# The fourth part of the modulation is loaded and summed during the two feed-forward layers instead of beside the values projection

## The reference

```
mod_l = silu(c) @ w_mod + b_mod                  # 6 parts of D = 2048: mod_l[0] .. mod_l[5]
hl    = modulate(rms_norm(xl, norm1_g), mod_l[0], mod_l[1])
zl    = hl @ w_in + b_in                         # projections: conv, sgu, q, k, v, gates
xl    = xl + mod_l[2] * mixer_output(...)
hl2   = modulate(rms_norm(xl, norm2_g), mod_l[3], mod_l[4])
xl    = xl + mod_l[5] * (relu(hl2 @ w_ff1 + b_ff1) ** 2 @ w_ff2 + b_ff2)
```

## Time and profile before

| | |
|---|---|
| median of 3 runs | 3076.25 us (3071.13 to 3077.77) |
| the profiled execution | 3078.38 us |
| its span on the core | 3076.6 us |
| PE busy | 3031.1 us (99%) |
| DVE busy | 1984.4 us (64%) |
| ACT busy, POOL busy | 331.5 us (11%), 63.3 us (2%) |
| DMA | 561.39 MB, 182 GB/s in the mean |
| chain that ended last | PE 88%, DVE 7%, DMA 4% |

### The profile page before, as it was taken

The page is one execution under the profiler, slowest core; times in us unless marked ns, Lnnn a source line. Parts: engine busy times, 40 slices in busy tenths (PEclk is TensorE's granted clock), DMA queues, the critical chain, the costliest instruction groups (busy, mean ns, idle before and its releaser), DMA issues.

```text
span 3076.6 us, 49684 instructions
## 1 busy us (share of the span) xinstructions
PE 3031.1 (99%) x21787; PEld 2725.3 (89%) x21787; DVE 1984.4 (64%) x2968; ACT 331.5 (11%) x643; POOL 63.3 (2%) x121
## 2 busy tenths in 40 slices
PE   6999999999999999999999999999999999999998
PEld 3688844498899999999999999999999998898998
DVE  1039975564256577766666777767667565996665
ACT  1021000022120000111110000001012102001010
POOL 0000000120000000000000000000000000000000
PEclk9999999999999999999999999999999999999999
DMA  7999977664345555755555555555445654554443
GB/s 273 308 310 299 293 245 279 224 189 131 124 138 174 169 178 178 188 166 165 192 165 165 165 165 170 170 157 189 138 143 160 198 174 124 155 145 110 123 150 111
DMA packets 580133, 561.39 MB, mean 182 GB/s; under 512 B 24317, under 2 KB 548176, under 8 KB 570445
## 3 DMA queue, kind: packets, MB, share of 16 engines
q1 hardware_dynamic: 550368, 466.65, 49.5%
q0 software_dynamic: 11552, 80.90, 7.2%
q10 hardware_dynamic: 17997, 10.67, 1.2%
HBM read 549.66 MB, written 8.51 MB: 181 GB/s over the span
## 4 chain that ended last, share of the span: by engine, by line
PE 88%; DVE 7%; DMA 4%; issue 0%; ACT 0%; SPq 0%; ACTq 0%; DVEq 0%; POOLq 0%
PE psum L487 39%; PE psum L467 20%; PE psum L764 4%; DVE arena L1954 3%; PE psum L627 2%; DVE arena L1902 2%; PE psum L565 2%; PE psum L895 2%; PE psum L883 2%; PE psum L893 2%; PE psum L888 2%; PE psum L894 2%; PE psum L885 2%; PE psum L880 2%; DMA arena<-w_mod 2%; DMA ring<-w_in 1%
## 5 line engine op out<-in xcount | busy, mean ns | idle before, releaser
L467 PE MATMUL psum<-arena,ring 128*128 128x256 f32 (+2 forms) x3712 | 870.0, 394 | 0.6 <-ACTq L1183 0.6
L467 PEld LDWEIGHTS psum<-arena,ring 128*128 128x128 f32 x3712 | 700.2, 190 | 157.0 <-issue 69.6
L487 PE MATMUL psum<-arena 128*128 128x128 f32 x6144 | 702.8, 275 | 0.3 <-DVE arena L1775 0.3
L487 PEld LDWEIGHTS psum<-arena 128*128 128x128 f32 x6144 | 694.4, 192 | 7.2 <-issue 6.2
L487 PE MATMUL psum<-arena,ring 128*128 128x128 f32 x4224 | 486.1, 275 | 0.0
L487 PEld LDWEIGHTS psum<-arena,ring 128*128 128x128 f32 x4224 | 479.1, 192 | 0.7 <-issue 0.5
L1763 DVE TENSOR_TENSOR arena<-ring 128x2048 f32<-128x2048 f32 x96 | 220.0, 2292 | 278.3 <-PE psum L487 275.9
L1902 DVE SCALAR_TENSOR_TENSOR arena<-arena,cvec 128x2048 f32<-128x2048 f32 x60 | 141.0, 2350 | 80.7 <-DMA arena<-w_mod 79.9
L1744 DVE TENSOR_TENSOR arena<-ring,arena 128x1024 f32<-128x1024 f32 (+1 forms) x168 | 167.3, 996 | 5.3
L1744 DVE TENSOR_TENSOR arena<-arena 128x512 f32<-128x512 f32 (+7 forms) x257 | 134.2, 522 | 16.2 <-DVE arena L2673 6.1
L2530 DVE TENSOR_TENSOR arena<-ring 128x1024 f32<-128x1024 f32 x64 | 78.4, 1225 | 90.3 <-PE psum L880 89.5
(11 more groups left out here) (335 smaller groups left out, 2953.4 us busy)
## 6 DMA issues: line engine op xcount, KB each, us to landing
ring<-w_ff SPq DMA_DIRECT2D x128, 1024.0 KB, 5.7
ring<-w_in SPq DMA_DIRECT2D x88, 1024.0 KB, 6.5
arena<-w_mod POOLq DMA_DIRECT2D x64, 1024.0 KB, 6.9
ring<-ab_w_in SPq DMA_DIRECT2D x56, 1024.0 KB, 5.6
ring<-cd_w_in SPq DMA_DIRECT2D x48, 1024.0 KB, 5.9
ring<-w_mod SPq DMA_DIRECT2D x32, 1024.0 KB, 7.3
ring<-w_in SPq DMA_DIRECT2D x32, 512.0 KB, 5.0
ring<-w_o SPq DMA_DIRECT2D x16, 1024.0 KB, 5.9
```

Source lines behind the costliest of these rows:

```text
L467: mm = pe.matmul(psum[:, s, m * N:(m + 1) * N], w[:, k, m * P:(m + 1) * P], x(k)[:, 0:N], start=(j == 0), stop=(j == kt - 1))
L487: return pe.matmul(o, z, w, **kw) if tokens else pe.matmul(o, w, z, **kw)
```

## The change

GpSimd's first loop loads 48 chunks instead of 64, VectorE's `chunks(16)` and its `mod_columns(3, 3)` are taken out of the place behind the values projection, and so is `mod_sum(3)` on TensorE. The fourth part is made later: each row k is loaded in two halves of 128x1024 (512 KB each) into `LATE_HALF`, and `add_late(k)` multiplies and adds the halves into `LATE`. Rows 0 to 11 follow the work of `tables` at p = 18 to 29, rows 12 to 15 follow turns i = 0 to 3 of the second feed-forward layer. TensorE's `mod_sum` for it stands behind step q = 9 of that layer, `mod_columns` at i = 5, and the bias work of p = 25 to 27 moves to i = 5 to 7. The new arrays lie where the tables of p = 17 lay, so GpSimd starts the first load only when their write to HBM has landed. The silu of c is copied to `cond` because `cvec` is overwritten in between.

```diff
-            for j in range(64):
+            for j in range(48):
...
             pool.dma_start(kept[1], at(36080, 4096)).then_inc(sem("load_tables_out"), 16)
+            pool.wait_ge(sem("load_tables_out"), 16)
+            for k in range(KT):
+                for h in range(2):
+                    pool.wait_ge(sem(f"chunk{h}_used"), n[f"chunk{h}_used"].next())
+                    c0 = 4096 + 3 * D + HW * h
+                    pool.dma_start(LATE_HALF[h], w[:, k, c0:c0 + HW]).then_inc(sem(f"load_chunk{h}"), 16)
             pool.wait_ge(sem("residual_made"), n["residual_made"].next())
             pool.dma_start(kept[0], at(0, 4096)).then_inc(sem("load_residual_out"), 16)
-            pool.wait_ge(sem("load_tables_out"), 16)
...
+            def add_late(k):
+                for h in range(2):
+                    v.wait_ge(sem(f"load_chunk{h}"), n[f"load_chunk{h}"].next())
+                    if k == 0:
+                        ins = v.tensor_scalar(LATE[:, h, :], LATE_HALF[h], cond[:, k:k + 1], None, ALU.mult)
+                    else:
+                        ins = v.scalar_tensor_tensor(out=LATE[:, h, :], in0=LATE_HALF[h], scalar=cond[:, k:k + 1],
+                                                     in1=LATE[:, h, :], op0=ALU.mult, op1=ALU.add)
+                    ins.then_inc(sem(f"chunk{h}_used"), n[f"chunk{h}_used"].up())
+                for h in range(2):
+                    v.wait_ge(sem(f"chunk{h}_used"), n[f"chunk{h}_used"].now())
+                if k == KT - 1:
+                    v.sem_inc(sem("mod_added"), n["mod_added"].up())
...
             mod_columns(2, 7)
-            chunk = chunks(16)
+            step(v.tensor_copy(cond[:, :], cvec[:, :, 0]))
             quarter_sums(HL, SM, "input_sums")
...
             pair_sums(0, w, TX)
-            mod_columns(3, 3)
...
-                elif p == 25:
-                    TT(gain[:, 1, :], mod[:, 80:96, 0], col("b_ff2", 0, KT), ALU.mult)
-                elif p in (26, 27):
-                    k = HT * (p - 26)
-                    TT(X[:, k:k + HT, :], X[:, k:k + HT, :], over(gain[:, 1, k:k + HT], T, 2), ALU.add)
+                if p >= 18:
+                    add_late(p - 18)
...
+                if i < 4:
+                    add_late(12 + i)
+                elif i == 5:
+                    mod_columns(3, 7, at(36080, KT, 32))
+                    TT(gain[:, 1, :], mod[:, 80:96, 0], col("b_ff2", 0, KT), ALU.mult)
+                elif i in (6, 7):
+                    k = HT * (i - 6)
+                    TT(X[:, k:k + HT, :], X[:, k:k + HT, :], over(gain[:, 1, k:k + HT], T, 2), ALU.add)
```

On TensorE the same four matmuls move:

```diff
-                            elif half == 1 and s == 3 and k == 2 and t == 0:
-                                mod_sum(3)
...
             for q in range(64):
                 hidden_slot(q)
+                if q == 9:
+                    mod_sum(7, LATE_ROWS)
```

More of the change, by code:

```diff
@@ L116 @@
 CHUNK_AT = (-4, -3, 0, 1, 2, 3, *(3 + g for g in CHUNK_PARTS), *(x - 12 for x in (39, 39, 39, 40, 40, 40, 42, 42, 42, 43, 43, 43, 44, 44, 44, 45, 45, 45,
-            46, 46, 46, 47, 48, 48, 48, 48, 49, 49, 49, 49, 50, 50, 50, 50, 51, 51, 51, 51)))
-assert len(CHUNK_AT) == 64
+            46, 46, 46, 47)))
+assert len(CHUNK_AT) == 48
 RECUR_VALUES = {9: 0, 11: 1, 13: 2, 15: 3, 25: 4, 27: 5, 31: 6, 33: 7}
@@ L182, in program @@
         glw = sb("glw", [P, KT, 32])
+        cond = sb("cond", [P, KT])
         small = sb("small", [P, 16])
@@ L224, in program @@
         BIAS = at(34032, NHEAD, 6, GRID)
-        MACC_ROWS = at(34032, KT, 4, 32)
+        MACC_ROWS, LATE_ROWS = at(34032, KT, 4, 32), at(36080, KT, 4, 32)
+        LATE, LATE_HALF = at(36080, 2, HW), [at(38128 + HW * h, HW) for h in range(2)]
         MACC, CHUNK = at(34032, D), [at(36080, D), at(38128, D)]
@@ L670, in _, with mod_sum @@
                     turn([(TAPN[0:TAPS, j * P:(j + 1) * P], 32 * j) for j in range(HT)], 4, "dve")
-            def mod_sum(b):
+            def mod_sum(b, rows=MACC_ROWS):
                 pe.wait_ge(sem("mod_added"), n["mod_added"].next())
@@ L677, in mod_sum @@
                 for i in range(4):
-                    mm = pe.matmul(psum[32 * i:32 * i + 32, b, :], ones[:, 0:32], MACC_ROWS[:, :, i, :], start=True,
+                    mm = pe.matmul(psum[32 * i:32 * i + 32, b, :], ones[:, 0:32], rows[:, :, i, :], start=True,
                                    stop=True)
@@ L1907, in add_chunk, with mod_columns @@
                     v.sem_inc(sem("mod_added"), n["mod_added"].up())
-            def mod_columns(i, b):
+            def add_late(k):
[11 more added lines that the diff above has]
+                    v.sem_inc(sem("mod_added"), n["mod_added"].up())
+            def mod_columns(i, b, own=at(34032, KT, 32)):
                 c = 32 + KT * i
                 v.wait_ge(sem(full("dve", b)), n[full("dve", b)].next())
-                own = at(34032, KT, 32)
                 v.tensor_tensor(own, psum[:, b, :].rearrange("p (k r) -> p k r", k=KT), over(diagonal[:, :], KT),
```

## The result

| | before | after |
|---|---|---|
| median | 3077.47 us (8 runs, 3071.13 to 3086.36) | 3086.87 us (8 runs, 3081.27 to 3088.47) |
| ratio, 95% interval | | 1.0026 [1.0017, 1.0036] |
| profiled execution, its span | 3078.38, 3076.6 us | 3086.8, 3085.0 us |
| PE busy | 3031.1 us (99%) | 3031.3 us (98%) |
| DVE busy | 1984.4 us | 1986.9 us |

The changed kernel is slower, by 8.0 us (5.2 to 11.1) if the ratio is laid on the median of before; the two medians differ by 9.4 us. The forecast was 3080.5 us with a range of 3075.3 to 3087.0: the time lies just inside its upper end, and outside the forecast's own range of 3076.8 to 3084.5. Of the distance to the forecast 1.2 us come from its starting point: it was laid on the median of three runs of before, 3076.25 us, and that of eight is 3077.47. A repetition beside other runs of before gave 3084.34 us, ratio 1.0022 [1.0012, 1.0032].

What follows compares the result with a forecast made beforehand. TensorE, busy in 99% of the span, bounds the kernel. 4.8 us of late first load plus 3.15 of long turns less 3.7 of margin gives 4.25, on 3076.25 us: 3080.5 us, range 3075.3 to 3087.

Steps and rivals of the forecast that it cites:

- The one mechanism, VectorE late behind the write of the tables: First feed-forward layer, p = 18 to 21: late first load and three long turns make TensorE wait 4.25 us.
- The landing of the halves: At p = 18: a 512 KB half lands 5.3 us after issue (2.5 to 8.3), making VectorE's turn 4.8 us late.
- The rival that a queue's order decides: At p = 18: queues served in issue order, halves 3.5 us later, sum about 8.5 us; no chance given.
- A row and the three long turns: p = 19 to 21: a row costs VectorE 2.45 us, turns take 13.56 us against TensorE's 12.51, 3.15 us late in all.
- The margin: First feed-forward layer, pair 20: VectorE's sums end 3.7 us before TensorE wants them, covering that much lateness.
- The pattern: TensorE's 4.25 us of waiting comes in four pieces, about 1.1, 1.05, 1.05 and 1.05 us, before pairs 20 to 23.
- The values projection, the moved matmuls: Work removed there is hidden except four matmuls, -1.06 us; they cost 1.06 us behind q = 9; sum 0.
- p = 22 and later: First feed-forward layer, p = 22 to 28: VectorE's 5.10 us idle per turn takes the 2.45 us row; lateness gone after two turns.
- the second layer: Row 11 lets `weight_sums(1)` end 2.3 us early; turns i = 0 to 3 have idle time for a row; all hidden.
- the ring: First feed-forward layer: the ring's weight loads stay in time for TensorE, though a turn moves 3.15 MB instead of 2.1.
- Loads late again and again: Rival: halves land over 11 us after issue, each row holds VectorE up; 3106 us, mild form 3087 to 3090; 14 in 100.
- Hidden: Rival: row 0 reaches VectorE by about 1507.7 us, so no loss or a little gain; 3076.3 or 3075.2 us; 16 in 100.

Runs made afterwards that it cites:

- no write: The changed kernel without the tables' write to HBM and the waits for it: 3077.76 us, ratio to before 1.0000.
- rows a turn later: The changed kernel with every row of the fourth part one turn later, row 0 behind p = 19: 3076.39 us, ratio to before 0.9997.
- write in two: The changed kernel with the 2 MB tables' write cut in two, the first halves loaded after the first part: 3081.58 us, ratio to before 1.0014.
- ring quiet: The changed kernel with the ring's two loads for pair 21 cut from 1 MB to 128 KB each: 3082.75 us, ratio to before 1.0015.

## Why the prediction was right or wrong

*The one mechanism, VectorE late behind the write of the tables: right, and it is the whole loss.* In the table above the whole loss follows the column "turn" over five kernels: 0.13, 1.17, 4.42, 4.74, 4.83 give 3.41, 4.43, 7.67, 7.99, 8.07, that is turn + 3.24 to 3.28 us each time, with a lower clock or without. And the rows without lateness (no write, rows a turn later) lose nothing.

*The landing of the halves: wrong in size, and this is the step that failed.* The prediction took 5.3 us, the median of whole chunks in the values projection, because the DMA share was alike in the mean (0.79 and 0.90). The half that counts took 8.1 us, near to its high end of 8.3, for which it gave a sum of 7.3 us; 8.07 was measured. The mean share of a stretch said nothing of the moment. The first halves are issued 2 us behind two loads of the ring, and the engines then move 368 GB/s at a share of 1.06, not 296 at 0.90. In each kernel whose halves are issued just behind the ring's two full loads they took 6.9 us or more, the run without the write among them; ahead of these loads (write in two) they took 5.2 and 6.2, and with the ring quiet 3.9 and 4.6. The trace of the kernel before could have told it, by the ring's own loads at that point of the turn:

```profile
L369 SPq DMA_DIRECT2D ring<-w_ff x2: 368/481/594, 1503.7 to 1504.1; - x2
...
DMA to landing us min/median/max: 6.5/7.7/8.9
```

So of the 8.10 us that the turn is late, against 4.8, 2.8 are this landing. Of the rest 0.3 is the write (it landed after 13.0 us instead of 12.1, but was issued 0.3 us sooner beside TensorE's work, and GpSimd woke 0.2 us faster), and 0.2 is the hand-over from the half to the turn (0.84 us instead of 0.65).

*The rival that a queue's order decides: not so.* It would have given about 8.5 us and comes near to the measured sum, but by another way. Landings of the ring's two loads ahead of the halves, in the kernel after:

```profile
L371 SPq DMA_DIRECT2D ring<-w_ff x2: 367/742/1116, 1502.8 to 1503.2; - x2
...
DMA to landing us min/median/max: 6.1/8.6/11.1
```

The load issued last at 1503.2 landed 11.1 us later, at 1514.3, behind both halves (1511.8 and 1513.5), which were issued 2 us after it. Each queue got its turns, and the ring's load paid too. The Trainium skill, page "DMA: Bandwidth & Descriptors", section "Queues, rings and completion order", says that an engine goes round between its queues; the two landings agree with it.

*A row and the three long turns, small misses:* a row costs 2.57 us (1525.46 to 1528.03) instead of 2.45, the turns 13.67 to 13.81 instead of 13.56, 3.63 us in all instead of 3.15. *The margin* of 3.7 us held: 8.10 + 3.63 - 3.7 = 8.03, where 8.07 was measured.

*The pattern: wrong for this run.* Four pieces of a microsecond were forecast; there was one of 4.34, one of 0.70, and 2.93 us at the lower clock, which no term of the prediction had. The lower clock changed where the time went, not how much: the 64 records at 0.50 used up the lateness of VectorE's next two turns.

*The values projection, the moved matmuls, p = 22 and later, the second layer, the ring:* right. -1.19 and +1.07 us instead of -1.06 and +1.06; no wait for `w_ff1` or `w_ff2` in TensorE's list; later halves land after 9.2 us at most and are wanted after 11. *Loads late again and again* did not happen. *Hidden* did not happen, but the run without the write shows how near it lay: the three rows alone are just covered.

*The span of 3080.85 us* that the prediction sets beside the 3078.38 us is the forecast one, 3076.6 + 4.25; that of before is 3076.6. The forecast time is not touched by it.

*The chances:* "within 0.2%" had 65 in 100, slower by more 32. Measured were 0.26% and 0.22%, just beyond the line. With the landing at 8 us the same sum would have been 7 us, and "slower" the likelier. That 3086.87 us still lies within the range of 3075.3 to 3087 is luck: the forecast's own range ended at 3084.5, and the upper end was drawn for late loads again and again, which did not happen.

What stays open: why the write of 2 MB takes 12 to 13 us (in the split run the first MB landed after 10.2 us and the second after 12.5), and why the lower clock cost 1.73 us in one profile of the kernel after and 2.93 in the other, behind nearly the same wait (4.08 and 4.17 us). Neither changes the sum.

## What to carry to other kernels

Take the landing of a new load from loads that were issued at the same point of the loop's turn, not from a mean over a stretch of like DMA share: here it was 4 us or 8, by whether the ring's loads had just been issued. Where a chain of write, load and use ends on an engine that feeds TensorE, move its first use one turn on; that alone took the change from 0.26% slower to no difference. And count lateness on the engine that is late: here the waits and the slower matmuls behind it were two faces of it, and to take one away gave back the other.

## What the runs showed of the hardware

TensorE's granted clock fell to 0.50 behind each of eight waits of 2.87 to 6.00 us, for 1.6 to 3.0 us of lost time, and stayed at 1.00 behind waits of 2.12 and 2.13 us. The loss did not grow steadily with the wait (2.9 us behind 4.54, 2.2 behind 6.00), and the clock didn't always fall at once: behind the wait of 2.99 us it was 0.92 in the mean from 1649.50 to 1651.00 and 0.50 from there to 1653.00. With matmuls into an unused psum buffer in place of a wait of about 4 us the clock stayed at 1.00. Two loads of 512 KB took 3.9 and 4.6 us with the ring quiet and 6.9 to 9.2 just behind its two loads, and a load of the ring took longer beside them: 11.1 us against the 8.9 of the longer one before.
